# One stage of head norms for both attentions of a mixer, and the memory keys moved into the first attention

## The reference, cut to what matters

```python
def odd_mixer(h, w_in, na_qk_gain, na_rpb, diff_qk_gain, ...):
    qc, kc, vc, qd, kd, vd = split_cols(h @ w_in, OD_SIZES)      # six times 512 columns
    qc = rms_norm(heads(qc, C_HEADS), na_qk_gain[0]) * (HEAD_DIM ** -0.5)
    kc = rms_norm(heads(kc, C_HEADS), na_qk_gain[1])
    yc = neighbourhood_attention(qc, kc, heads(vc, C_HEADS), na_rpb)
    q12 = rms_norm(pair_heads(qd), diff_qk_gain[0]) * (D_QK_DIM ** -0.5)
    k12 = rms_norm(pair_heads(kd), diff_qk_gain[1])
    yd = differential_attention(q12[0], q12[1], k12[0], k12[1], heads(vd, D_HEADS), lam, t5_table)
    yd = rms_norm(yd, diff_gain.reshape(D_HEADS, 1, D_V_DIM)) * (1.0 - lam_init)
    return jnp.concatenate([merge(yc), merge(yd)], axis=-1) @ w_out

def memory_cross_attention(h, m, w_q, w_kv, qk_gain, w_o):       # m = rms_norm(mem, norm_mem[l])
    q = rms_norm(heads(h @ w_q, CA_HEADS), qk_gain[0]) * (CA_HEAD_DIM ** -0.5)
    k, v = jnp.split(m @ w_kv, 2, axis=-1)
    k = rms_norm(heads(k, CA_HEADS), qk_gain[1])
    ...
```

## Time and profile before

| | |
|---|---|
| median of 3 runs | 2405.51 us (2404.97 to 2410.62) |
| the profiled execution | 2403.74 us, its span 2401.9 us |
| mean granted clock of TensorE | 0.968 |
| busy, share of the span | PE 94%, PEld 90%, DVE 63%, ACT 45%, POOL 15% |
| chain that ended last | PE 83%, DVE 9%, ACT 5%, issue 2% |

### The profile page before, as it was taken

How to read it: one execution, slowest core, us unless ns; L and a number is a source line. 1 busy time by engine, 2 the same in 40 slices (tenths; PEclk the granted TensorE clock), 3 DMA queues, 4 the chain that set the end, 5 groups by cost and what they waited for, 6 DMA issues and landing times.

```text
span 2401.9 us, 40464 instructions
## 1 busy us (share of the span) xinstructions
PE 2264.0 (94%) x17516; PEld 2157.3 (90%) x17516; DVE 1502.5 (63%) x2186; ACT 1081.5 (45%) x1285; POOL 350.4 (15%) x300
## 2 busy tenths in 40 slices
PE   7988899998789999999999899999999999899998
PEld 6878799997679999999998798999999988788998
DVE  5566687843467878667756547667656556556665
ACT  4445544534455445335336355335334236445333
POOL 1680000045000000000535110000000015310000
PEclk9999999998899999999999799999999999989999
DMA  8663255543234554555643344455555643344552
GB/s 244 178 169 105 97 178 200 161 157 106 70 106 168 181 196 159 194 175 175 186 127 109 113 162 155 162 201 173 186 177 176 161 146 108 106 158 132 181 203 91
DMA packets 314660, 374.28 MB, mean 156 GB/s; under 512 B 23127, under 2 KB 280931, under 8 KB 313331
## 3 DMA queue, kind: packets, MB, share of 16 engines
q1 hardware_dynamic: 309283, 353.83, 45.5%
q0 software_dynamic: 3424, 11.50, 1.7%
q10 hardware_dynamic: 1776, 6.37, 0.8%
HBM read 362.49 MB, written 9.18 MB: 155 GB/s over the span
## 4 chain that ended last, share of the span: by engine, by line
PE 83%; DVE 9%; ACT 5%; issue 2%; POOL 0%; DMA 0%; ACTq 0%; DVEq 0%
PE banks L857 23%; PE banks L860 22%; PE banks L858 22%; PE banks L885 3%; PE banks L886 3%; PE banks L889 3%; DVE wlo L1752 2%; ACT whi L1335 2%; PE banks L1113 1%; PE banks L1151 1%; PE banks L1137 1%; PE banks L1033 1%; PE banks L1020 1%; DVE x_lo L1810 1%; PE banks L867 1%
## 5 line engine op out<-in xcount | busy, mean ns | idle before, releaser
L857 PE MATMUL banks<-x_hi,wlo 128*128 128x256 f32 (+1 forms) x4344 | 1110.0, 288 | 39.7 <-DVE wlo L1752 15.4
L858 PE MATMUL banks<-x_lo,whi 128*128 128x256 f32 (+1 forms) x4344 | 1098.5, 285 | 0.0
L1335 ACT ACTIVATE whi<-raw 128x2048 fp32r<-128x2048 f32 (+1 forms) x340 | 637.3, 1878 | 680.0 <-PE banks L860 617.6
L857 PEld LDWEIGHTS banks<-x_hi,wlo 128*128 128x128 f32 (+1 forms) x4344 | 843.6, 194 | 60.5 <-issue 34.2
L858 PEld LDWEIGHTS banks<-x_lo,whi 128*128 128x128 f32 (+1 forms) x4344 | 844.5, 194 | 1.0 <-issue 1.0
L1752 DVE TENSOR_TENSOR wlo<-raw,whi 128x2048 fp32r<-128x2048 f32 (+2 forms) x292 | 658.3, 2264 | 170.7 <-ACT whi L1335 170.4
L860 PE MATMUL banks<-x_hi,whi 128*128 128x256 f32 x4344 | 691.9, 285 | 0.0
L860 PEld LDWEIGHTS banks<-x_hi,whi 128*128 128x128 f32 x4344 | 599.6, 194 | 3.6 <-issue 0.9
L825 POOL TENSOR_TENSOR wlo<-raw,whi 128x512 fp32r<-128x512 f32 x184 | 239.7, 1340 | 1173.9 <-ACT whi L1335 1173.9
L885 PE MATMUL banks<-x_hi,wlo 128*128 128x256 f32 (+1 forms) x632 | 177.1, 312 | 31.5 <-DVE gt L1786 11.6
L886 PE MATMUL banks<-x_lo,whi 128*128 128x256 f32 (+1 forms) x632 | 169.1, 299 | 0.0
(11 more groups left out here) (254 smaller groups left out, 1966.3 us busy)
## 6 DMA issues: line engine op xcount, KB each, us to landing
raw<-in_ffn_w_gu SPq DMA_DIRECT2D x88, 1024.0 KB, 5.2
raw<-in_ffn_w_down SPq DMA_DIRECT2D x66, 1024.0 KB, 5.1
raw<-in_ffn_w_up SPq DMA_DIRECT2D x44, 1024.0 KB, 5.1
raw<-in_w_in SPq DMA_DIRECT2D x42, 1024.0 KB, 5.3
raw<-in_ca_w_kv SPq DMA_DIRECT2D x16, 1024.0 KB, 5.3
raw<-in_od_w_in SPq DMA_DIRECT2D x12, 1024.0 KB, 5.1
raw<-in_ev_w_in SPq DMA_DIRECT2D x10, 1024.0 KB, 6.2
raw<-in_w_in SPq DMA_DIRECT2D x20, 512.0 KB, 5.1
```

What stands on the lines that cost most here:

```text
L857: eng.matmul(out, a[1], b[0], start=first and i == 0, stop=False, skip_group_check=True)
L858: eng.matmul(out, a[0], b[1], start=False, stop=False, skip_group_check=True)
L1335: eng.activation(whi[s % SETS][:, 0:ch["n"]], raw[i % SLOTS][:, 0:ch["n"]], ACT.Copy).then_inc(S["weights_hi"], 1)
```

## The change

The linear stage takes the queries and keys of both attentions (8 units). The four value units are the fillers N[0] to N[3]. One stage of head norms takes all 8 groups: the 16 rows of the first four groups use columns 0 to 255 of the bank and of the root's tiles, those of the other four columns 256 to 511. N[0] to N[2] are its fillers, N[3] stands in front of the neighbourhood attention's barrier. In that attention the memory chunk is rounded behind N[3], K[0] stands in slot 1 and K[1] in slot 3. K[2] stands in front of the differential attention's barrier, K[3] and the H units where they were. The output of the differential attention goes to tiles 0 to 3 of `ft`, and the memory keys of this layer to tiles 16 to 19; the cross attention is told so. One stage and its barrier fall away.

```diff
@@ odd_mixer
-            linear(features(w, b, 0, 1024, 0) + values(w, b, 1024, 512, 0), norm=norm, join=True, tokens=True, spread=True)
-            N = enroll(features(w, b, 1536, 1024, 8) + values(w, b, 2560, 512, 512))
+            linear(features(w, b, 0, 1024, 0) + features(w, b, 1536, 1024, 8), norm=norm, join=True, tokens=True, spread=True)
+            N = enroll(values(w, b, 1024, 512, 0) + values(w, b, 2560, 512, 512))
-            heads_norm([(t, 2, na + t // 4) for t in (0, 2, 4, 6)], HD, "rows_odd", fill={"pre": (N[1], N[0]), 0: (N[2], N[1]), 1: (N[3], N[2])})
+            heads_norm([(t, 2, na + t // 4) for t in (0, 2, 4, 6)] + [(8 + t, 2, df + t // 4) for t in (0, 2, 4, 6)], HD, "rows_odd",
+                       fill={"pre": (N[1], N[0]), 0: (N[2], N[1]), 1: (N[3], N[2])})
+            K = memory_units(1, b, N[3], 16)
             attention("softmax", [small_heads(o, 0, 4, (h, h + 1), 0, 0, bias=lambda h: na_bias[:, h], tables=True) for h in range(0, 8, 2)],
-                      fill={0: (N[4], N[3]), 1: (N[5], N[4]), 2: (N[5] + 1, N[5]), 3: (N[5] + 1, N[5] + 1)})
-            K = memory_units(1, b, N[5])
+                      fill={"pre": (N[3] + 1, N[3], 1), 0: (N[3] + 1, N[3] + 1, 2), 1: (K[1], K[0]), 3: (K[2], K[1])})
             H = enroll(residual_half(wo, o, 0))
-            stages[-1]["fill"][4] = (N[5] + 1, N[5] + 1, 3)
-            heads_norm([(8 + t, 2, df + t // 4) for t in (0, 2, 4, 6)], HD, "rows_odd",
-                       fill={"pre": (K[1], K[0]), 0: (K[2], K[1]), 1: (K[3], K[2])}, after=n_of["att"])
             attention("difference", [head(ft[:, 8 + h, :], ft[:, 12 + h, :], 0, P, vt[:, :, 512 + h * P:512 + (h + 1) * P],
-                                          ft[:, 16 + h, :], bias=t5_bias[:, h]) for h in range(4)],
-                      fill={0: (K[3] + 1, K[3]), 1: (H[1] + 1, K[3] + 1), 2: (H[2] + 1, H[2])})
+                                          ft[:, h, :], bias=t5_bias[:, h]) for h in range(4)],
+                      fill={"pre": (K[3], K[2]), 0: (K[3] + 1, K[3]), 1: (H[1] + 1, K[3] + 1), 2: (H[2] + 1, H[2])})
...
@@ heads_norm
-            row = 0
+            row, half = 0, 0
             for i, (t, n, gain) in enumerate(groups):
-                groups[i] = dict(x=ft[:, t:t + n, :], n=n, gain=gain, row=row)
+                if row + n * (P // d) > HEAD_ROWS:
+                    row, half = 0, half + 1
+                groups[i] = dict(x=ft[:, t:t + n, :], n=n, gain=gain, row=row, first=row == 0, columns=slice(half * SEQ, (half + 1) * SEQ))
                 row += n * (P // d)
...
@@ heads, TensorE
-                        m = eng.matmul(post_bank[0][0:R, 0:SEQ], C(f"to_row{st['d']}", at, R), wk[:, i % 4, t * SEQ:(t + 1) * SEQ],
-                                       start=i == 0 and t == 0, stop=last)
+                        m = eng.matmul(post_bank[0][0:R, g["columns"]], C(f"to_row{st['d']}", at, R), wk[:, i % 4, t * SEQ:(t + 1) * SEQ],
+                                       start=g["first"] and t == 0, stop=last)
...
@@ norms_of_heads, ScalarE (VectorE's root likewise)
-                y = rstd[0:R, 0, 0:SEQ]
+                y = rstd[0:R, 0, 0:W]
```

More of the change, by code:

```diff
@@ L413, in residual_half, with memory_units, memory_keys @@
             return residual_part(w, buf, half, 0) + residual_part(w, buf, half, 1)
-        def memory_units(layer, buf, last_unit):
+        def memory_units(layer, buf, last_unit, tile):
             c = mem_chunk(layer, buf, last_unit, pool=True)
             wkv = io["ca_w_kv"][layer]
-            us = enroll(features(wkv, buf, 0, 512, 0, "plain")) + enroll(values(wkv, buf, 512, 512, 0, "plain"))
+            us = enroll(features(wkv, buf, 0, 512, tile, "plain")) + enroll(values(wkv, buf, 512, 512, 0, "plain"))
             units_of[us[0]]["memory"] = c
             return us
-        def memory_keys(layer):
-            return [(t, 2, prow["ca_gain"] + layer) for t in (0, 2)]
+        def memory_keys(layer, tile):
+            return [(t, 2, prow["ca_gain"] + layer) for t in (tile, tile + 2)]
         def make_parts(src, n, buf, tile, made, per=1, by=None, scale=1.0):
@@ L437, in heads_norm @@
         def heads_norm(groups, d, rows, rope=None, gates=None, **more):
-            row = 0
+            row, half = 0, 0
             for i, (t, n, gain) in enumerate(groups):
-                groups[i] = dict(x=ft[:, t:t + n, :], n=n, gain=gain, row=row)
+                if row + n * (P // d) > HEAD_ROWS:
+                    row, half = 0, half + 1
+                groups[i] = dict(x=ft[:, t:t + n, :], n=n, gain=gain, row=row, first=row == 0, columns=slice(half * SEQ, (half + 1) * SEQ))
                 row += n * (P // d)
-            stage("heads", groups=groups, spread=n_of.get("mixer", 0), d=d, rows=row, scale=rows, rope=rope, gates=gates, n=number("heads"),
+            for g, following in zip(groups, groups[1:] + groups[:1]):
+                g["last"] = following["first"]
+            stage("heads", groups=groups, spread=n_of.get("mixer", 0), d=d, rows=HEAD_ROWS if half else row, width=(half + 1) * SEQ, scale=rows, rope=rope, gates=gates, n=number("heads"),
                   g0=number("norm_group", len(groups)), r0=number("rope_group", len(groups) if rope else 0), **more)
@@ L516, in even_mixer @@
                       tanh={6: M[7] + 1})
-            heads_norm([(18 + h, 1, prow["ev_mlstm_gain"] + h) for h in range(4)] + memory_keys(0), P, "rows_cell",
+            heads_norm([(18 + h, 1, prow["ev_mlstm_gain"] + h) for h in range(4)] + memory_keys(0, 0), P, "rows_cell",
                        fill={"pre": (H[3], H[2]), 0: (H[3] + 1, H[3] + 1)})
@@ L543, in odd_mixer, with cross_attention @@
             return linear(residual_half(wo, o, 1), parts=parts, then=then, join=True)[-1]
-        def cross_attention(norm, then, wq, wo):
+        def cross_attention(norm, then, wq, wo, ktile):
             b = norm["buf"]
             us = linear(features(wq, b, 0, 512, 4), norm=norm, join=True)
-            attention("softmax", [large_head(b, 4, 0, h) for h in range(4)], join=True, queries=dict(units=us, n=number("queries", 2), tile=4))
+            attention("softmax", [large_head(b, 4, ktile, h) for h in range(4)], join=True, queries=dict(units=us, n=number("queries", 2), tile=4))
@@ L664, in build @@
             nm, now = fold(prow["norm_ffn"] + 8 * l, 1 - b), nm
-            cross_attention(now, nm, io["ca_w_q"][l], io["ca_w_o"][l])
+            cross_attention(now, nm, io["ca_w_q"][l], io["ca_w_o"][l], 16 * (l % 2))
             nm, now = fold(prow["norm_mix"] + 8 * (l + 1) if l + 1 < DEPTH else prow["ffn1_norm_2"], 1 - b), nm
@@ L1032, in heads @@
                         onto = spread[0:R, r * HD:(r + per) * HD] if st["d"] == HD else ident[0:R, r:r + 1].to_broadcast([R, P])
-                        m = eng.matmul(banks[i % 4][:, t * SEQ:(t + 1) * SEQ], onto, rstd[0:R, 0, 0:SEQ], start=True, stop=True)
+                        m = eng.matmul(banks[i % 4][:, t * SEQ:(t + 1) * SEQ], onto, rstd[0:R, 0, g["columns"]], start=True, stop=True)
                     m.then_inc(S["qk_spread"], 1)
@@ L1488, in norms_of_heads @@
             def norms_of_heads(st):
-                g0, R = st["g0"], st["rows"]
+                g0, R, W = st["g0"], st["rows"], st["width"]
                 for i, g in enumerate(st["groups"]):
```

16 lines of the change are left out of this document (8 added, 8 removed).

## The result

The changed kernel takes 2409.07 us, the median of 20 runs (2408.43 to 2416.49); the kernel before takes 2404.62 in 20 runs beside it (2398.77 to 2413.77). The ratio is 1.0020, 95% interval [1.0012, 1.0028]: slower by 4.5 us, less than the 0.3% that I set as the bound of a difference. The forecast was 2408.5. The profiled execution took 2411.11 us.

What follows compares the result with a forecast made beforehand. TensorE, busy 83%, was taken to bound the kernel, so only its idle or slow time counts. Reordering -0.7, clock 2.3 and 1.3, GpSimd 0.2 gave +3.1 us on the profiled execution, so 2408.5 us against the median 2405.51; range 2404 to 2412.

Steps and rivals of the forecast that it cites:

- the wait moved and a few us of clock: Odd mixer: TensorE's idle time only moves and some clock is lost; the forecast itself, 2408.5 us, chance 0.68.
- Steps 1 to 4: Linear stage, joined norm stage, barriers and fillers: two more units 11.5 us, squares 7.1, spreading 7.3, roots hidden behind N[1].
- Step 5: Neighbourhood attention: the first key unit waits for the memory activations' rounding and split, 12.3 us after N[3], TensorE idle 8.5.
- Step 6: K[0] after the idle wait takes 8.2 us as before; then attention products 5.2, K[1] 5.94, values and turn 2.0.
- Step 7: Tail of the neighbourhood attention without filler: waits of 1.7 and 1.1 us, together with its products 5.8 us.
- Sum without new clock falls: From 506.60 us to the first differential scores: 95.7 us against 96.4, so -0.7.
- Step 9: Slow clock: 2.3 us lost at the joined spreading (bounds 0 and 3.65), 1.3 at the tail, 0 at the squares.
- Step 10: GpSimd's string beside VectorE's normalising: VectorE pays at most 5 us within TensorE's wait, GpSimd 0.2 (bounds 0 and 1.1).
- The scores of the differential attention: Sign of a right forecast: these scores start at 602 to 608 us; before 597 us would show it wrong.
- The clock holds: Rival: no clock fall in the norms or at the tail, 3.6 us less, 2404.9 us; chance 0.13.
- Slower, by the clock: Rival: squares and spreading both at half clock, K[0] and K[2] slow too; +9.9 us, 2415.4 us; chance 0.12.
- The fillers cover the gaps: Rival: key units fill TensorE's idle time in the attention, about -15 us against before, 2390.5 us; chance 0.07.

Runs made afterwards that it cites:

- e3: The changed kernel with memory units K[0] and K[1] in slots 2 and 4 of the neighbourhood attention instead of 1 and 3; 2406.9 us, ratio 1.0003 to the kernel before.
- e5: The changed kernel with the joined norm stage's spreading padded by zero rows to 128 contraction rows, result unchanged; 2406.45 us, ratio 1.0 to the kernel before.
- e7: The kernel before with the spreading padded by zero rows in the odd mixer's two norm stages of 64 features; 2402.2 us, ratio 0.9982 to the kernel before.
- e9: The kernel before with the spreading padded by zero rows to 128 contraction rows in every stage of head norms; 2396.22 us, ratio 0.9951 to the kernel before.
- e2: The changed kernel with the joined spreading contracting over 128 rows of ones instead of 16, norms not the reference's; 2404.09 us, ratio 0.9995 to the kernel before.
- e1: The changed kernel with filler N[2] moved between the two halves of the norms' spreading; 2412.39 us, ratio 1.0017 to the kernel before.

## Why the prediction was right, and where it was not

The time was right (2408.5 against 2409.07), and so was the likeliest case: the wait moved and a few us of clock. That it came so near is partly luck: the forecast adds 3.0 us to 2405.51, while the kernel before took 2404.62 in the runs beside, and the medians differ by 4.5. Step by step:

- *Steps 1 to 4* (linear stage, barriers, squares, roots behind N[1]): every step has its length, the roots stayed hidden behind N[1] as taken, and no clock fall came of L1020 (L1022 now: 7.01 us against the 7.1 taken, clock 1.00). The window table is hidden: it begins at 555.97 and ends before the first scores.
- *Step 5*, the new wait: 8.5 us predicted, 8.5 measured. It is not all loss: e3 gets 3.7 of it back, the rest is bound by the string of ScalarE, GpSimd and VectorE, which the old order had too.
- *Step 6*, K[0]: 8.2 predicted, 8.38 at 0.68.
- *Step 7*, the tail: waits of 1.7 and 1.1 predicted; 2.5 together measured, the longer 1.3.
- *Sum without new clock falls*: -0.7 and 0.2 for GpSimd predicted; e5 against the kernel before gives -1.9. In the prediction's sum stand 1.6 us for the old patch of slow clock; without them it has +1.1 for the change itself. That e5 against e7 has +1.05 is a chance agreement, since e7 gained 3.0 and not 1.6; the traces of e7 and e9 put the change at 0.3 to 1.8 us of cost up to the differential scores. In no pair of orders do the timed runs show a gain.
- *Step 9*, the clock, was the term that was mis-sized, and its upper bound was wrong. I took 2.3 us for the joined spreading, at most 3.65, "the whole stretch at half". It lost 5.1 (5.8 by e5), since the fall does not end with the products that it follows: it began 4.2 us after their start at 537.2 and went on through the first 4.5 us of N[2]. A fall costs by its own length, not by that of the stretch. The trace of before had a row against the bound that step 9 left out. There are five stretches of L1033, not four, and only those at 522.3 and 591.5 have 16 contraction rows (the one at 74.6 has 12, the others 8). The fifth, at 649.0, has no more than 16 products, and the clock stood at 0.50 for 10.2 us from 650.6 on. For the tail I took 1.3 and lost nothing; K[2] ran at 1.00 (581.88 to 606.92). So 5.8 stand against 3.6, and -1.9 against -0.5: the total, +3.9 against +3.1, is near because the two errors partly cancel.
- *Step 10*: GpSimd nearly nothing, 0.2 (10.05 against 9.87 in the earlier trace rows); VectorE "at most 5", 4.84. "SBUF — State Buffer" of the Trainium skill (section "SBUF: two separate sides"), the lock whose loser blocks fully: on VectorE the trace agrees (4.84 against 1.14), of GpSimd it does not, whose 8 operations lost 0.2 us to VectorE's 4, not 1.1.
- *The scores of the differential attention* start at 606.92; 602 to 608 was predicted (the sum gives 606.1).
- *The rivals.* "The clock holds" is what e2 and e5 make of the kernel: 2404.09 and 2406.45, where 2404.9 was worked out. "Slower, by the clock" had the spreading nearer to right (3.65 lost, against 5.1) and the squares, K[2] and GpSimd wrong. "The fillers cover the gaps" was rightly ruled out by the earlier trace rows.

The rule of "TensorE: Matmul & The Clock Gate" of the Trainium skill (section "Why this matters for your kernels"), that a TensorE kept busy keeps its clock, is contradicted again for these products: it was busy for all of the 10.20 us from 541.40 at 0.50, and for the whole of the spreading before that; the same products with 128 contraction rows kept it at 1.00 (e2, e5).

What stays open: how much the falls outside the odd mixer are worth one by one. The padding everywhere brings 0.31%, 0.31% and 0.27% in three pairs of kernels, each pair taken over two sessions by its ratios to the kernel before, but single traces differ by several us in the first 480 us whatever the kernel. Open too is what sets the length of a fall: the one at 649.0, behind 16 products over 8 rows, was as long as that at the joined stage's 32 over 16.

## What to carry to other kernels

A stage of matmuls with few contraction rows is dearer than its own time: look at the granted clock behind it, and where the unused rows can be zeros, fill them. That gave 0.5% here, where the reordering gave nothing. Before a filler is placed where TensorE idles, follow the string that makes its operands; a filler that is not ready becomes the wait itself, with all that is queued behind it.

## What the runs showed of the hardware

- With 16 contraction rows and 128 output rows, 7.3 us of products together were followed by 10.2 us at 0.50; two halves with a unit between by 3.4 and 6.8 (e1). With 128 rows, zeros or not, by none (e2, e5). The 16 products over 8 rows at 649.0 before had a fall of 10.2 us among and behind them. Padded to 128 rows and behind 2.7 us of idle time, they still had a fall of 3.4 us among them (e9, 648.0). Products over 128 contraction rows with only 16 output rows (L1022, 7.0 us) did not lower it.
- Padding cost no time of its own: 32 products with 128 rows took 7.07 us in e5, 16 with 16 rows 3.65 in the earlier trace rows.
- Four operations of VectorE (128x256) took 1.14 us alone, 2.84 with GpSimd beside the first 2.2 of them, 4.84 wholly beside it; GpSimd's eight took 10.05 instead of 9.87.
